# Delta rule inputs of a two-block model: two small sums computed with the data as moving columns in four column groups

## The chip, the cores and the metric

The kernel is one program on one core of a Trainium2 chip. The metric is the device time of one execution in microseconds (us); the median of several executions is what is compared. TensorE is called PE below, VectorE DVE, ScalarE ACT, GpSimd POOL, and the sync engine, which issues the weight loads, SP.

## The reference, cut to what matters

The reference is a block of two layers followed by a second block of two layers, on 256 tokens of width 1024. The part that matters here is the gated delta rule in the second layer of the first block:

```
proj = xn @ od_w_in[i]                       # 1024 -> 3080 columns
z, qkv, gate, b_raw, a_raw = jnp.split(proj, OD_SPLITS, axis=-1)   # b_raw, a_raw: 4 columns each
qkv = jax.nn.silu(causal_dwconv(qkv, conv_w))
q = l2norm(split_heads(q, DN_HEADS, DN_HEAD_DIM)) * DN_HEAD_DIM ** -0.5   # 4 heads of 128 channels
k = l2norm(split_heads(k, DN_HEADS, DN_HEAD_DIM))
beta = jax.nn.sigmoid(b_raw)
g = -jnp.exp(a_log) * jax.nn.softplus(a_raw + dt_bias)
o = chunked_gated_delta_rule(q, k, v, g, beta)
# l2norm(t) = t * rsqrt(sum(t * t, axis=-1) + 1e-6)
```

Two small results are at stake. The first is `xn @ od_w_in[:, 3072:3080]`, eight columns per token, the raw beta and decay inputs. The second is the sum of squares over the 128 channels of each head of q and of k, eight numbers per token.

## The kernel before

Activations lie channel-major: `xnT` is 8 tiles of 128 channels by 256 tokens, `d_cv` is 12 such tiles (4 of q, 4 of k, 4 of v). Tokens come in two tiles of 128 (`t` in `range(TT)`). Results that are needed per token as a scalar (beta, decay, norms) lie with the token on the partition, in the small table `small`.

Large products go through the weights in units of 4096 columns, loaded by SP into a ring of two places, and each unit in pieces of 512 columns. For each piece ACT writes a rounded copy (`w_hi`, `round_weights`), POOL writes the remainder (`w_lo`, `remainders`), and PE multiplies high by high, low by high, and, after the remainder is there, high by low. Four pieces are held at once (`HELD`), and ACT may round piece p only when PE has started piece p - 3 (`piece_started`). The units around the change are, in this order, `odq`, `odk`, `odv` (channel-major, the inputs of q, k and v), then `ozv`, `ozu`, `odg` (token-major). In the token-major routine `split_token_major` the argument `second_half` is work put in before piece 2, and `after` is work put in before piece 4.

Each engine's program is written out by hand in one order, and engines wait for each other by semaphores: `B.take` waits until a PSUM bank is emptied, `B.wait_full` until PE has filled it, and `DA`/`DV` name steps of ACT and DVE. Around the change the orders are:

- PE: `odk`, the 16 matmuls "ba" (8 moving columns each, L1198, into bank 4), 4 transposes of the spatial gating weights (L1203, bank 5), `odv`, `ozv` pieces 0 to 3, `square_sums` (16 matmuls of one moving column, L1162, bank 4, and 4 of eight, "gc", L1167, bank 5), `ozv` pieces 4 to 7, `ozu` pieces 0 and 1, `rows_a` (L1175, waits for DVE's step "diag_a"), and on.
- ACT: `odv` pieces 0 to 2, silu of q (`silu(0)`, L1922), `last_tap(1)` (the convolution's last tap of k, read from PSUM through L1670), the sigmoid of beta (L1936), `odv` pieces 3 to 7, `silu(1)`, `ozv` 0 and 1, the pieces of the softplus (L1942 to L1948) with `ozv` 2 and 3 between, `last_tap(2)`, `ozv` 4 to 6, the copies of "gc" (L1954), the logarithm of the sums of squares (L1956, step "rates"), `ozv` 7, `ozu` 0, the exponential of the factors (L1962, which waits for DVE's step "logs"), `ozu` 1 and on.
- DVE: `convolution(1)` (L2514 scales the banks, L2521 adds three taps, 12 instructions), the shift of the decay input, the masked spatial weights, the squares of q and k (L2544, step "squares"), the decay g, `convolution(2)`, then the sums of squares plus epsilon (L2552), and a chain of small operations to the step "logs" (L2567).

In both small sums the data is the stationary operand: a 128x128 tile of `xnT` or of `d_sq` is loaded into PE, and the 8 weight columns or one column of ones move through it. So each result lands with tokens on partitions. All these are full float32 matmuls, and the profile keeps two records for each.

## Time and profile before

| what | us |
|---|---|
| three executions | 2037.42, 2040.48, 2041.2 |
| their median | 2040.48 |
| the profiled execution | 2043.08 |
| its span in the trace | 2041.3 |
| PE busy in it | 2003.6 |
| POOL busy in it | 1621.6 |
| ACT busy in it | 1088.5 |
| DVE busy in it | 862.6 |
| "ba" matmuls (L1198), busy | 4.7 |
| squares matmuls (L1162), busy | 3.6 |

The trace spans 2041.3 us of the 2043.08 us that this execution took, so 1.8 us lie around it. A PE row's length is from issue to the modelled end, so rows that follow each other overlap; the distance between the starts of two rows is what a row costs when PE never waits. The granted clock of PE is 1.00 where it runs at 2.4 GHz and 0.50 at 1.2 GHz; over the span it is 0.992.

### The profile page before, as it was taken

The numbers are of one execution on the slowest core, as the hardware profiler recorded it, in microseconds if no ns is written. First come the engines' busy times: TensorE is split into PE (matmuls) and PEld (weight loads), VectorE is DVE, ScalarE is ACT, GpSimd is POOL, SyncE is SP. The second block draws the span as 40 slices with busy tenths as digits, with TensorE's granted clock in tenths as the row PEclk, the third lists the DMA queues.
The fourth block names the chain that finished last, engine by engine and source line by source line (L and its number), as shares of the span: only waits on it lengthen the run. The fifth ranks groups of instructions, "written<-read, shape, count | busy, mean of one in ns | idle before, by whom it ended". The sixth has DMA issues, their size and how long they took to land.

```text
span 2041.3 us, 32301 instructions
## 1 busy us (share of the span) xinstructions
PE 2003.6 (98%) x12383; PEld 1752.5 (86%) x12383; DVE 862.6 (42%) x2024; ACT 1088.5 (53%) x2124; POOL 1621.6 (79%) x1272
## 2 busy tenths in 40 slices
PE   9999999999999999999999989999999999999998
PEld 8798999898888999898788858888997788678886
DVE  4412565056522466082413273553432412644541
ACT  4454666456354566444554585544444544865443
POOL 6685898977395898999889518999997896268997
PEclk9999999999999999999999999999999999999999
DMA  9753555553053676565456604655554557135553
GB/s 308 149 181 123 186 186 176 184 172 104 21 186 124 198 234 199 181 191 186 145 183 192 209 2 165 204 188 186 183 189 145 165 188 231 63 125 175 190 200 107
DMA packets 244271, 343.14 MB, mean 168 GB/s; under 512 B 8819, under 2 KB 172755, under 8 KB 243989
## 3 DMA queue, kind: packets, MB, share of 16 engines
q1 hardware_dynamic: 231832, 330.83, 49.2%
q10 hardware_dynamic: 12285, 10.24, 2.5%
q8 instruction: 99, 1.62, 0.3%
q14 instruction: 55, 0.45, 0.1%
HBM read 336.85 MB, written 4.19 MB: 167 GB/s over the span
## 4 chain that ended last, share of the span: by engine, by line
PE 90%; DVE 3%; ACT 3%; POOL 1%; issue 1%; DMA 1%; DVEq 0%; POOLq 0%; SPq 0%; ACTq 0%
PE bank L774 9%; PE bank L781 9%; PE bank L777 9%; PE bank L824 8%; PE bank L830 8%; PE bank L827 8%; PE bank L796 7%; PE bank L854 5%; PE bank L857 5%; PE bank L861 5%; PE bank L801 4%; DVE E L2305 1%; POOL w_lo L1572 1%; PE bank L1367 1%; DVE E L2291 1%
## 5 line engine op out<-in xcount | busy, mean ns | idle before, releaser
L1572 POOL TENSOR_TENSOR w_lo<-ring,w_hi 128x512 fp32r<-128x512 f32 (+1 forms) x1216 | 1575.1, 1314 | 368.0 <-ACT w_hi L1670 330.4
L1670 ACT ACTIVATE w_hi<-ring 128x512 fp32r<-128x512 f32 (+1 forms) x1216 | 757.8, 630 | 786.2 <-PE bank L824 261.5
L774 PE MATMUL bank<-x_pair,w_hi 128*128 128x256 f32 x1504 | 380.7, 285 | 2.3 <-DVE x_pair L2191 1.5
L777 PE MATMUL bank<-x_pair,w_hi 128*128 128x256 f32 x1504 | 378.0, 283 | 0.0
L824 PE MATMUL bank<-w_hi,x_pair 128*128 128x512 f32 (+1 forms) x752 | 299.4, 398 | 2.9 <-issue 1.9
L827 PE MATMUL bank<-w_hi,x_pair 128*128 128x512 f32 (+1 forms) x752 | 293.8, 391 | 0.0
L774 PEld LDWEIGHTS bank<-x_pair,w_hi 128*128 128x128 f32 x1504 | 289.4, 192 | 5.0 <-issue 1.5
L777 PEld LDWEIGHTS bank<-x_pair,w_hi 128*128 128x128 f32 x1504 | 289.4, 192 | 0.4
L781 PE MATMUL bank<-x_pair,w_lo 128*128 128x256 f32 x1504 | 242.1, 283 | 0.0
L830 PE MATMUL bank<-w_lo,x_pair 128*128 128x512 f32 (+1 forms) x752 | 232.7, 391 | 1.4 <-POOL w_lo L1572 1.3
L781 PEld LDWEIGHTS bank<-x_pair,w_lo 128*128 128x128 f32 x1504 | 207.9, 192 | 0.0
L854 PE MATMUL bank<-w_hi,hidden 128*128 128x512 f32 x480 | 187.2, 390 | 0.0
L857 PE MATMUL bank<-w_hi,hidden 128*128 128x512 f32 x480 | 186.8, 389 | 0.0
L796 PE MATMUL bank<-x_pair,w_hi 128*128 128x512 f32 x640 | 174.7, 394 | 0.0
L824 PEld LDWEIGHTS bank<-w_hi,x_pair 128*128 128x128 f32 x752 | 144.2, 192 | 32.9 <-issue 5.4
L830 PEld LDWEIGHTS bank<-w_lo,x_pair 128*128 128x128 f32 x752 | 142.6, 192 | 33.0 <-POOL w_lo L1572 4.3
L827 PEld LDWEIGHTS bank<-w_hi,x_pair 128*128 128x128 f32 x752 | 144.2, 192 | 27.8 <-issue 0.7
L861 PE MATMUL bank<-w_lo,hidden 128*128 128x512 f32 x480 | 147.8, 389 | 0.0
L796 PEld LDWEIGHTS bank<-x_pair,w_hi 128*128 128x128 f32 x640 | 109.4, 189 | 14.7
L2183 DVE TENSOR_TENSOR h<-bank,h 128x512 f32<-128x512 f32 x36 | 23.1, 685 | 209.4 <-PE bank L861 153.6
L801 PEld LDWEIGHTS bank<-x_pair,w_lo 128*128 128x128 f32 x640 | 98.2, 189 | 13.6
L854 PEld LDWEIGHTS bank<-w_hi,hidden 128*128 128x128 f32 x480 | 90.1, 188 | 18.8 <-issue 0.4
(333 smaller groups left out, 2422.0 us busy)
## 6 DMA issues: line engine op xcount, KB each, us to landing
ring<-in_w_in SPq DMA_DIRECT2D x74, 1024.0 KB, 5.0
ring<-in_ffn_w_up SPq DMA_DIRECT2D x44, 1024.0 KB, 5.1
ring<-in_w_ffn_in SPq DMA_DIRECT2D x44, 1024.0 KB, 5.1
ring<-in_ffn_w_down SPq DMA_DIRECT2D x20, 1024.0 KB, 4.9
ring<-in_w_ffn_out SPq DMA_DIRECT2D x20, 1024.0 KB, 5.0
ring<-in_xattn_wkv SPq DMA_DIRECT2D x16, 1024.0 KB, 5.3
ring<-in_w_o_ret SPq DMA_DIRECT2D x16, 1024.0 KB, 5.0
ring<-in_od_w_in SPq DMA_DIRECT2D x12, 1024.0 KB, 5.2
```

The costliest lines, as they stand in the source:

```text
L774: m = mm(out_, view(w_hi)[:, k, :], x_hi[:, 4 * kh + k, :], start=start, stop=False)
L777: mm(out_, view(w_hi)[:, k, :], x_lo[:, 4 * kh + k, :], start=False, stop=False)
L781: m = mm(out_, view(w_lo)[:, k, :], x_hi[:, 4 * kh + k, :], start=False, stop=stop)
L796: m = mm(bank[b][:, :], view(w_hi)[:, k, :], x_pair[:, 4 * kh + k, :, :].rearrange("p a n -> p (a n)"), start=kh == 0 and k == 0, stop=False)
L824: m = mm(acc, hi, view(w_hi), start=k == 0, stop=False)
L827: mm(acc, lo, view(w_hi), start=False, stop=False)
L830: m = mm(bank[b0 + t][:, 0:n], x_hi[:, k, t * P:(t + 1) * P], view(w_lo), start=False, stop=k == KT - 1)
L854: m = mm(bank[b][:, :], hi, view(w_hi), start=kt == 0, stop=False)
L857: mm(bank[b][:, :], lo, view(w_hi), start=False, stop=False)
L861: m = mm(bank[b][:, :], x_hi[:, kt, t * P:(t + 1) * P], view(w_lo), start=False, stop=kt == tiles - 1)
L1572: tt(view(w_lo), src, view(w_hi), ALU.subtract).then_inc(w_lo_ready, 1)
L1670: return A(o, i_, ACT.Copy, **kw)
```

## The change

Both sums are turned round: the data moves, the small operand is stationary. A stationary tile of 32 columns fills one of the four column groups of PE, so that its result lands on 32 partitions of the bank (partitions 32c to 32c+31 for group c), 256 tokens wide. Eight channel tiles go through in two rounds of four groups, and the second round adds to the first.

- "ba": 8 matmuls of 32 stationary by 256 moving columns ("baT", L1209 in the new numbering) leave four partial sums in bank 4. ACT copies the bank to `d_baT` (which lies in `d_kb`, unused at that point). After the 4 transposes of the spatial weights, 2 matmuls (L1219) take `d_baT` as stationary and a matrix `fold`, which has a one for every partition with the same number modulo 32, as 8 moving columns: this adds the four groups and turns the result to tokens on partitions, in the layout of before.
- squares: 8 matmuls ("ssT", L1164) with a 32-column window of `sel` that holds a single column of ones, so that group c gets the sums of head c of q on its first partition and of k on its second. They are issued before `ozv` piece 2 in place of piece 4. ACT copies the bank to `d_ssT` between `ozv` piece 3 and `last_tap(2)`. Before piece 4 PE transposes the two halves back (L1172), and "gc" follows as before. DVE then reads the eight columns with a stride, in two instructions for one (L2581).
- DVE fills `sel` and the spare columns of `wba` at the start and builds `fold` from the identity by three additions in the first layer. `wba` and `sel` take 96 more float32 columns of SBUF.

```diff
-        wba = sb("wba", [P, KT, 8])
+        wba = sb("wba", [P, KT * 8 + 32])
+        sel = sb("sel", [P, 64])
...
+        d_ssT, d_baT = (d_kb[:, 2 * j:2 * j + 2, :].rearrange("p a b -> p (a b)") for j in range(2))
+        fold = sel[:, 40:48]
...
             def square_sums():
                 pe.wait_ge(*DV.after("squares"))
+                B.take(pe, "ssT", 4)
+                for r in range(2):
+                    for c in range(4):
+                        m = mm(bank[4][32 * c:32 * c + 32, 0:SEQ], sel[:, 1 - r:33 - r], d_sq[:, 4 * r + c, :], start=r == 0, stop=r == 1)
+                m.then_inc(full[4], 1)
+            def turn_sums():
+                B.wait_emptied(pe, "ssT")
                 B.take(pe, "ss", 4)
-                for a in range(8):
-                    for t in range(TT):
-                        c = (a // 4) * 8 + t * 4 + a % 4
-                        m = mm(bank[4][:, c:c + 1], d_sq[:, a, t * P:(t + 1) * P], c_ones[:, 0:1], start=True, stop=True)
+                for t in range(TT):
+                    m = tr(bank[4][:, t * P:(t + 1) * P], d_ssT[:, t * P:(t + 1) * P], ident[:, :])
                 m.then_inc(full[4], 1)
...
-            B.take(pe, "ba", 4)
-            for t in range(TT):
-                for k in range(KT):
-                    m = mm(bank[4][:, t * 8:(t + 1) * 8], xnT[:, k, t * P:(t + 1) * P], wba[:, k, :], start=k == 0, stop=k == KT - 1)
+            B.take(pe, "baT", 4)
+            for r in range(2):
+                for c in range(4):
+                    k = 4 * r + c
+                    m = mm(bank[4][32 * c:32 * c + 32, 0:SEQ], wba[:, 8 * k:8 * k + 32], xnT[:, k, :], start=r == 0, stop=r == 1)
             m.then_inc(full[4], 1)
...
+            B.wait_emptied(pe, "baT")
+            B.take(pe, "ba", 4)
+            for t in range(TT):
+                m = mm(bank[4][:, t * 8:(t + 1) * 8], d_baT[:, t * P:(t + 1) * P], fold, start=True, stop=True)
+            m.then_inc(full[4], 1)
             channel_major("odv", x_parts)
-            token_major("ozv", x_parts, after=square_sums)
+            token_major("ozv", x_parts, second_half=square_sums, after=turn_sums)
...
             silu(0)
+            evacuate("baT", d_baT)
             last_tap(1)
...
             round_weights("ozv", HELD - 1, HELD)
+            evacuate("ssT", d_ssT)
             last_tap(2)
...
-            ts(small[:, 20:22, :].rearrange("p a b -> p (a b)"), bank[4][:, 0:16], EPS, None, ALU.add).then_inc(empty[4], 1)
+            sums_of = bank[4][:, 0:SEQ].rearrange("p (t a j) -> p t a j", t=2, a=4)
+            for r in range(2):
+                m = ts(small[:, 20 + r, :].rearrange("p (t a) -> p t a", t=2), sums_of[:, :, :, r], EPS, None, ALU.add)
+            m.then_inc(empty[4], 1)
```

In the order listings below, line numbers of the new kernel are 3 higher than before in the piece routines (L777 is the old L774, L784 the old L781, L827, L830 and L833 the old L824, L827 and L830); a row's name is the tile, and a count with x says how often it follows itself.

PE between `odk` and `odv`, before:

```order
L781 MATMUL bank<-x_pair,w_lo 128x256 x3
L1198 MATMUL bank<-wba,xnT 128x8 [waits bank_empty4,xn_ready]
L1198 MATMUL bank<-wba,xnT 128x8 x15
L1203 MATMUL bank<-ident,PT 128x128 [waits params_loaded,bank_empty5]
L1203 MATMUL bank<-ident,PT 128x128 x3
L774 MATMUL bank<-x_pair,w_hi 128x256 [waits w_hi_ready,bank_empty2]
```

PE at the same place, now:

```order
L784 MATMUL bank<-x_pair,w_lo 128x256 x3
L1209 MATMUL bank<-xnT,wba 32x256 [waits bank_empty4,xn_ready]
L1209 MATMUL bank<-xnT,wba 32x256 x7
L1214 MATMUL bank<-ident,PT 128x128 [waits params_loaded,bank_empty5]
L1214 MATMUL bank<-ident,PT 128x128 x3
L1219 MATMUL bank<-sel,region 128x8 [waits bank_empty4]
L1219 MATMUL bank<-sel,region 128x8
L777 MATMUL bank<-x_pair,w_hi 128x256 [waits w_hi_ready,bank_empty2]
```

Sixteen matmuls of 8 columns became eight of 256 in front of the transposes and two of 8 behind them, and those two wait for ACT's copy (`bank_empty4`).

PE between `ozv` piece 3 and piece 4, before:

```order
L830 MATMUL bank<-w_lo,x_pair 128x512 [waits w_lo_ready]
L830 MATMUL bank<-w_lo,x_pair 128x512
L1162 MATMUL bank<-region 128x1 [waits bank_empty4,dn_dve_steps]
L1162 MATMUL bank<-region 128x1 x15
L1167 MATMUL bank<-small,region 128x8 [waits bank_empty5,dn_dve_steps]
L1167 MATMUL bank<-small,region 128x8 x3
L824 MATMUL bank<-w_hi,x_pair 128x512 [waits w_hi_ready]
```

PE between `ozv` piece 1 and piece 2, now:

```order
L833 MATMUL bank<-w_lo,x_pair 128x512 [waits w_lo_ready]
L833 MATMUL bank<-w_lo,x_pair 128x512
L1164 MATMUL bank<-region,sel 32x256 [waits bank_empty4,dn_dve_steps]
L1164 MATMUL bank<-region,sel 32x256 x7
L827 MATMUL bank<-w_hi,x_pair 128x512 [waits w_hi_ready]
```

PE between `ozv` piece 3 and piece 4, now:

```order
L833 MATMUL bank<-w_lo,x_pair 128x512 [waits w_lo_ready]
L833 MATMUL bank<-w_lo,x_pair 128x512
L1172 MATMUL bank<-ident,region 128x128 [waits bank_empty4]
L1172 MATMUL bank<-ident,region 128x128
L1177 MATMUL bank<-small,region 128x8 [waits bank_empty5,dn_dve_steps]
L1177 MATMUL bank<-small,region 128x8 x3
L827 MATMUL bank<-w_hi,x_pair 128x512 [waits w_hi_ready]
```

The wait for the squares (`dn_dve_steps`) moved two pieces forward, and two transposes stand where sixteen one-column matmuls stood.

ACT from the silu of q to the sigmoid of beta, before:

```order
L1922 ACTIVATE region<-region 128x1024 [waits dn_dve_steps]
L1670 ACTIVATE region<-bank,vecs 128x256 [waits dn_dve_steps]
L1670 ACTIVATE region<-bank,vecs 128x256 x3
L1936 ACT_TABLE_LOAD
L1936 ACTIVATE small<-bank,rstd 128x4 [waits bank_full4]
```

ACT at the same place, now (L1938 is the old L1922, L1686 the old L1670, L1953 the old L1936):

```order
L1938 ACTIVATE region<-region 128x1024 [waits dn_dve_steps]
L1794 ACTIVATE region<-bank 128x256 [waits bank_full4]
L1686 ACTIVATE region<-bank,vecs 128x256 [waits dn_dve_steps]
L1686 ACTIVATE region<-bank,vecs 128x256 x3
L1953 ACT_TABLE_LOAD
L1953 ACTIVATE small<-bank,rstd 128x4 [waits bank_full4]
```

The copy of the new sums stands in front of the last tap of k.

## Rows read from the trace of the kernel before

**Rows 1.** The page's shares of the chain that ended last.

```profile
PE 90%; DVE 3%; ACT 3%; POOL 1%; issue 1%; DMA 1%; DVEq 0%; POOLq 0%; SPq 0%; ACTq 0%
```

**Rows 2.** PE's timeline, "ba" to `odv` piece 4: start, us, engine, line, operation, tiles, shape, count.

```profile
430.96 4.74 PE L1198 MATMUL bank<-wba,xnT 128*128 128x8 f32 x32
435.55 1.09 PE L1203 MATMUL bank<-ident,PT 128*128 128x128 f32 x4
436.30 0.56 PE L774 MATMUL bank<-x_pair,w_hi 128*128 128x256 f32 x1
...
443.80 0.28 PE L774 MATMUL bank<-x_pair,w_hi 128*128 128x256 f32 x1
```

**Rows 3.** Windows: stretch, us, busy of PE, PEld, DVE, ACT, POOL, clock, DMA, GB/s.

```profile
433.30:440.10 6.80, 6.80 (x34) 6.80 (x34) 6.20 (x17) 3.08 (x6) 1.28 (x1) 0.50 0.04 7
...
460.50:464.00 3.50, 3.50 (x10) 2.75 (x9) 2.73 (x13) 3.46 (x6) 1.37 (x2) 0.51 0.00 0
1112.00:1122.00 10.00, 9.71 (x98) 8.61 (x97) 1.34 (x2) 4.03 (x7) 7.66 (x7) 1.00 0.64 201
```

**Rows 4.** PE's timeline at a burst of 16 matmuls with 32 stationary columns (L1390).

```profile
1115.34 0.64 PE L781 MATMUL bank<-x_pair,w_lo 128*128 128x256 f32 x4
1115.91 1.93 PE L1390 MATMUL bank<-ring,E 128*32 128x256 f32 x32
1118.13 0.36 PE L774 MATMUL bank<-x_pair,w_hi 128*128 128x256 f32 x1 [0.29 <-issue]
```

**Rows 5.** ACT's timeline, last tap of k (in brackets the idle time before).

```profile
431.89 1.57 ACT L1670 ACTIVATE region<-bank,vecs 128x256 f32<-128x256 f32 x4 [0.48 <-DVE bank L2514]
```

**Rows 6.** PE's timeline from `ozv` piece 0 to `rows_a`, beginnings of pieces.

```profile
449.56 0.40 PE L824 MATMUL bank<-w_hi,x_pair 128*128 128x512 f32 x1
...
452.61 0.39 PE L824 MATMUL bank<-w_hi,x_pair 128*128 128x512 f32 x1
...
455.33 3.63 PE L1162 MATMUL bank<-region 128*128 128x1 f32 x32
458.82 1.04 PE L1167 MATMUL bank<-small,region 128*128 128x8 f32 x8
459.71 0.49 PE L824 MATMUL bank<-w_hi,x_pair 128*128 128x512 f32 x1
...
465.50 0.39 PE L824 MATMUL bank<-w_hi,x_pair 128*128 128x512 f32 x1
...
466.87 0.39 PE L824 MATMUL bank<-w_hi,x_pair 128*128 128x512 f32 x1
...
469.59 1.88 PE L1175 MATMUL bank<-region 128*128 128x512 f32 x4
```

**Rows 7.** DVE's timeline: taps of k, squares, taps of v.

```profile
433.50 5.10 DVE L2521 SCALAR_TENSOR_TENSOR region<-bank,vecs,region 128x255 f32<-128x255 f32 x12 [1.64 <-ACT region L1670]
...
447.16 2.29 DVE L2544 TENSOR_TENSOR region<-region 128x2048 f32<-128x2048 f32 x1 [7.13 <-ACT region L1922]
...
457.24 5.10 DVE L2521 SCALAR_TENSOR_TENSOR region<-bank,vecs,region 128x255 f32<-128x255 f32 x12 [1.64 <-ACT region L1670]
```

**Rows 8.** ACT's timeline: `ozv` pieces 4 to 6, piece 7 with `ozu` 0, `ozu` 1 and 2.

```profile
457.08 1.68 ACT L1670 ACTIVATE w_hi<-ring 128x512 fp32r<-128x512 f32 x3
...
463.00 1.13 ACT L1670 ACTIVATE w_hi<-ring 128x512 fp32r<-128x512 f32 x2
...
466.58 0.22 ACT L1962 ACTIVATE small<-small 128x24 f32<-128x24 f32 x1 [1.15 <-DVE small L2567]
466.71 1.14 ACT L1670 ACTIVATE w_hi<-ring 128x512 fp32r<-128x512 f32 x2
```

**Rows 9.** POOL's timeline, the remainders of the same pieces.

```profile
457.80 3.76 POOL L1572 TENSOR_TENSOR w_lo<-ring,w_hi 128x512 fp32r<-128x512 f32 x3 [3.43 <-ACT w_hi L1670]
463.69 2.54 POOL L1572 TENSOR_TENSOR w_lo<-ring,w_hi 128x512 fp32r<-128x512 f32 x2 [2.13 <-ACT w_hi L1670]
467.41 4.88 POOL L1572 TENSOR_TENSOR w_lo<-ring,w_hi 128x512 fp32r<-128x512 f32 x3 [1.18 <-ACT w_hi L1670]
```

More of the change, by code:

```diff
@@ L1515, in load_constants @@
                 sp.dma_start(e_poolw, I["pool_w"][0].rearrange("g c d -> c g d")).then_inc(const_loads, 16)
-                sp.dma_start(wba[:, :, :], I["od_w_in"][0][:, 3072:3080].rearrange("(k p) n -> p k n", p=P)).then_inc(const_loads, 16)
+                sp.dma_start(wba[:, 0:KT * 8].rearrange("p (k n) -> p k n", n=8), I["od_w_in"][0][:, 3072:3080].rearrange("(k p) n -> p k n", p=P)).then_inc(const_loads, 16)
                 sp.dma_start(dn_row[:, 0, :], I["dn_dt_bias"].broadcast_to([P, 4])).then_inc(const_loads, 16)
@@ L2340, in _ @@
             nc.vector.memset(nothing[:, :].bitcast(F32), 0.0).then_inc(nothing_ready, 1)
+            nc.vector.memset(wba[:, KT * 8:KT * 8 + 32], 0.0)
+            nc.vector.memset(sel[:, :], 0.0)
+            drain()
+            nc.vector.memset(sel[:, 1:2], 1.0)
             nc.vector.memset(cmpbias[:, 0, CMP_SEEN:N_CMP, :].rearrange("p b c -> p (b c)"), -FAR)
@@ L2371, in _ @@
             tt(g_both[:, :], vecs[:, r0:r0 + KT], vecs[:, r1:r1 + KT], ALU.mult)
+            tt(fold, ident[:, 0:8], ident[:, 32:40], ALU.add)
+            drain()
+            tt(fold, fold, ident[:, 64:72], ALU.add)
+            drain()
+            tt(fold, fold, ident[:, 96:104], ALU.add)
             for t in range(TT):
```

## The prediction

> **What bounds the kernel now.** I read the chain that ended last first: PE holds 90% of it [rows 1], so a microsecond that PE saves counts if nothing else steps in. Then I read PE's timeline around the two sums. The sum "ba" takes from 430.96 to 435.55, so 4.59 us, and the transposes 0.75 us more, until `odv` piece 0 at 436.30 [rows 2]. The sum of squares takes from 455.33 to 458.82, 3.49 us, and "gc" 0.89 us, until `ozv` piece 4 at 459.71 [rows 6]. Third, the windows of the granted clock: it is 0.50 (1.2 GHz) from 433.3 to 440.1 and 0.51 from 460.5 to 464.0 [rows 3]. So PE falls to its lower level 2.3 us after "ba" begins, and again right behind the squares and "gc": both times PE had done matmuls with 1 or 8 moving columns for more than 2 us, and it rose again only after dense work. What the falls cost: `odv` pieces 0 to 3 take from 436.30 to 443.80, 7.50 us [rows 2], where the next four take 5.76 us, from 443.80 to 449.56 [rows 2, 6], that is 1.44 each. So 1.74 us are lost. `ozv` pieces 4 to 6 take 5.79 us from 459.71 to 465.50, where a piece at full clock takes 1.37 (465.50 to 466.87) [rows 6]. So 1.68 us are lost.
>
> Fourth, I read who else is close behind. ACT and DVE go through a long chain for the delta rule in the same stretch: its steps are paced by each other and not by PE. That chain decides how much of PE's saving stays.
>
> **What a burst in four column groups costs.** The trace has the same form, 128 by 32 stationary and 256 moving columns in float32, at L1390: 16 matmuls, 32 records. The piece before it has its last four matmuls from 1115.34, at 0.12 us each (a piece of 1.44 us has twelve), so PE would have gone on at 1115.82; it goes on with the next piece at 1118.13 [rows 4]. The 16 cost 2.31 us, of which 1.93 us lie in the records, 0.06 us each, and some 0.4 us are the gaps ahead of and behind them. Eight matmuls with their 16 records cost 2.31 - 0.96, so 1.35 us. The Trainium skill (TensorEngine Tiling (Array Packing), Key Properties) says that a change of tiling mode drains TensorE; the trace agrees, with gaps of 0.09 and 0.29 us. The clock stays at 1.00 over the ten microseconds around this burst [rows 3], so I take the new bursts as no cause of a fall.
>
> **First place, "ba".** New times in before's own scale. PE starts baT at 430.96 and is free for the transposes at 432.3. These took 0.75 us at half clock [rows 2]; at full clock at least half of that, and I take 0.45, to 432.75. ACT is free at 431.41 (it idled 0.48 us before 431.89) [rows 5] and copies the bank when it is full, at about 432.4; 256 columns take it 0.39 us (1.57 for four) [rows 5], so until 432.8 to 432.9. There the fold starts: it has four records, and "gc" has eight in 0.89 us [rows 6], so 0.45 us. With 0.1 us for the hand-over PE starts `odv` at 433.45 in place of 436.30: 2.85 us earlier. The transposes hide all but 0.1 to 0.2 us of the round trip over ACT; without that cover it would cost 0.5 us more. With a clock that doesn't fall, `odv` piece 4 starts 5.76 us later, at 439.2 in place of 443.8. **The first place gives 2.85 + 1.74, so 4.6 us** at `odv` piece 4.
>
> The copy stands ahead of the last tap of k, which ends at 434.5 in place of 433.46, so the taps of k on DVE (5.1 us) [rows 7] end near 439.6, 1 us later. Who waits for that is the silu of k. ACT reaches it behind `odv` piece 7, which is tied to the start of `odv` piece 4 and so comes near 440.2. It is on time with 0.6 us to spare. The sigmoid of beta follows 1 us later, and ACT then rounds `odv` piece 3 until 436.7, where PE asks for it at 433.45 + 4.32, so 437.8. Both fit.
>
> **Second place, the squares.** From `odv` piece 4 on (call its start S, 443.80 before) ACT's and DVE's chain keeps its distances: `odv` piece 7, silu of k, `ozv` 0 and 1, softplus, decay, taps of v, logarithm. So I count from S. The squares are ready at S + 5.65 (447.16 + 2.29) [rows 7] and PE asks for them at `ozv` piece 2, S + 8.8 (452.61) [rows 6], with 3.2 us to spare. PE does the burst until S + 10.15, pieces 2 and 3 until S + 12.9, two transposes in 0.25 (about half of the four above), "gc" in 0.89, and starts piece 4 at S + 14.05, where it was S + 15.9; its high part is there at 457.08 + 0.56, S + 13.84 [rows 8], and for its remainder (457.80 + 1.25, S + 15.25) [rows 9] PE waits 0.3 us. ACT's copy of ssT falls in a wait of ACT for the scaled bank of v, and costs nothing. PE asks for piece 7 at S + 18.45 (three pieces of 1.37 on, and the 0.3). But ACT rounds piece 7 behind the logarithm, which needs the sums plus epsilon, which DVE does behind the taps of v (457.24 to 462.3) [rows 7]: the high part is there at 463.00 + 0.56, S + 19.76 [rows 8], and the remainder at 463.69 + 1.27, S + 21.16 [rows 9]. None of that comes sooner by the change; the earlier "gc" and the second DVE instruction (under 0.2 us) about cancel. PE waits 1.3 us for the high part and, after its four high matmuls of 0.91 us, 0.5 us for the remainder. It starts `ozu` at S + 21.65, where it was S + 23.07 [rows 6]: 1.4 us earlier. `ozu` piece 0 ends at S + 23.0. Piece 1 is rounded behind the exponential that waits for DVE's "logs", at 466.71 + 0.57, S + 23.5 [rows 8], and its remainder comes at 467.41 + 1.3 to 1.6, S + 24.9 to 25.2 [rows 9]. PE waits 0.5 and then 0.5 to 0.8 us and reaches `rows_a` at S + 25.35 to 25.7, where it was S + 25.79 (469.59) [rows 6]. **So the second place gives 0.1 to 0.44, I take 0.35 us.** Of its 1.85 us of direct saving and 1.68 us of clock nearly all becomes waiting.
>
> **The rest.** The fills of `sel` and `fold` lie where DVE waits for PE in the first layer, and cost nothing there. Behind `rows_a` DVE's, ACT's and PE's work have all moved by 4.6 to 5, so nothing new waits. **Sum: 4.6 + 0.35, so 5.0 us.** The profiled execution (2043.08, of which 2041.3 is the span) would become 2038.1. The three executions have a median 2.6 us below it, and I make the sum against that median too: 2040.48 - 5.0, so 2035.5 us. A spread of 3.8 us between them says that the time at the lower clock isn't the same in each; where the fall was shorter, less can be won.
>
> **Rivals.**
>
> *PE is the bound all through.* If ACT's and DVE's chain comes sooner than I count (its order leaves some starts to PE), the second place gives 3.49 - 1.35 - 0.25 = 1.89 us and 1.68 us of clock. Together 4.6 + 3.6 = 8.2 us, 2032.3 us. For it speaks that PE hardly idles in the stretch; against it, the time of rounding of piece 7, 1.9 us ahead of its use before (463.56 against 465.50) [rows 6, 8], less than what is saved. 15%.
>
> *The clock falls at the first place all the same.* PE goes 2.5 us without a dense piece, and the fall before came 2.3 us after "ba" began. Then `odv` starts at 433.7 and runs at half speed for half to all of the 6.4 us up to 440.1, which loses 1.6 to 3.2 us. At S 2.6 + 1.74 - 1.6 to 3.2, so 1.1 to 2.7 us are left, with the second place 1.5 to 3.1: 2037.4 to 2039.0 us, I take 2038.4. Against it stands the burst at L1390, 2.3 us long and with the clock at 1.00 [rows 3, 4]. The Trainium skill (TensorE: Matmul & The Clock Gate, Part 4: PE-mode transpose) says that a transpose doesn't count as busy for the clock; that would speak for this rival, since four of them stand between the burst and the fold. By that rule the time is this rival's, by the rows of L1390 the forecast's. 17%.
>
> *Slower, from the moved tiles.* `wba` and `sel` push all that is allocated behind them (the region with the attention's and the delta rule's tiles, `hidden`) by 96 float32. If ACT and DVE work on moved tiles became slower, it would show in the 6% of the chain that are theirs [rows 1], 122 us: 4% of it cancels the gain, and 8% costs 9.8 us, so 4.8 us net, 2045.3 us. The ring, `w_hi` and `w_lo`, on which the pieces rest, are allocated ahead of `wba` and don't move, and 384 bytes keep every alignment up to 128. 4%.
>
> **How the numbers follow.** The forecast has 64%. Differences under 0.2%, 4.1 us, can't be told from no change here. The forecast is 5.0 us, close to that line, with 1 us of doubt in its terms and the spread of the executions on top: 46 of its 64 I count as faster, 18 as the same. The first rival is faster (15), the second the same but for 2 (15 and 2), the third slower (4). So faster 0.63, same 0.33, slower 0.04. The range runs from under the first rival (2031.5) to above the upper end of the second (2039.4).
>
> **What would show it.** Right: the two bursts of 16 records last 1 us each and `odv` piece 0 starts 2.9 us sooner with the clock at 1.00 up to the end of `ozv`; PE rows of `ozv` piece 7 and `ozu` piece 1 name ACT or POOL as what ended 0.5 to 1.4 us of idle time; `rows_a` comes some 5 us sooner and everything after it by as much. Wrong: a clock of 0.5 anywhere from 430 to 470; no idle time in front of `ozv` piece 7 (the first rival); PE waiting in front of the fold, or for the squares at `ozv` piece 2; attention's DVE and ACT rows of the second block longer than before.

## The result

| | median us | lowest to highest | executions |
|---|---|---|---|
| kernel before | 2040.48 | 2035.28 to 2043.26 | 11 |
| changed kernel | 2044.73 | 2042.27 to 2046.59 | 11 |

The ratio is 1.0027, with a 95% interval of 1.0017 to 1.0037: the change makes the kernel slower by 3.5 to 7.5 us. The forecast was 2035.5 us in a range of 2031.5 to 2039.4, so the sign is wrong. What makes this case worth reading is that nearly every row which the prediction told the reader to look at came out as forecast. The loss is in other places.

**The two places of the change.** This is PE's timeline of the changed kernel around "ba", the rows that answer to [rows 2] (start, us, engine, line, operation, tiles, shape, count, idle time before and what ended it):

```profile
430.99 1.07 PE L1209 MATMUL bank<-xnT,wba 128*32 128x256 f32 x16
431.99 0.66 PE L1214 MATMUL bank<-ident,PT 128*128 128x128 f32 x4
432.65 0.58 PE L1219 MATMUL bank<-sel,region 128*128 128x8 f32 x4
433.09 0.36 PE L777 MATMUL bank<-x_pair,w_hi 128*128 128x256 f32 x1
...
444.68 0.40 PE L827 MATMUL bank<-w_hi,x_pair 128*128 128x512 f32 x1
```

The burst takes 1.0 us (430.99 to 431.99), the transposes 0.66, the fold 0.44, one right behind the other, and `odv` begins 2.10 us after the burst's start, where it took 5.34. The first piece of `ozv` starts at 444.68 in place of 449.56, 4.9 us sooner. And further on, what answers to [rows 6]:

```profile
448.02 1.07 PE L1164 MATMUL bank<-region,sel 128*32 128x256 f32 x16
449.02 0.50 PE L827 MATMUL bank<-w_hi,x_pair 128*128 128x512 f32 x1
...
451.88 0.38 PE L1172 MATMUL bank<-ident,region 128*128 128x128 f32 x2
452.09 0.96 PE L1177 MATMUL bank<-small,region 128*128 128x8 f32 x8
453.04 0.50 PE L827 MATMUL bank<-w_hi,x_pair 128*128 128x512 f32 x1
...
454.41 0.74 PE L833 MATMUL bank<-w_lo,x_pair 128*128 128x512 f32 x2 [0.18 <-POOL w_lo L1588]
...
458.81 0.50 PE L827 MATMUL bank<-w_hi,x_pair 128*128 128x512 f32 x1 [0.89 <-ACT w_hi L1686]
...
460.17 0.73 PE L833 MATMUL bank<-w_lo,x_pair 128*128 128x512 f32 x2 [0.16 <-POOL w_lo L1588]
...
462.52 0.50 PE L827 MATMUL bank<-w_hi,x_pair 128*128 128x512 f32 x1 [0.25 <-ACT w_hi L1686]
...
464.02 0.73 PE L833 MATMUL bank<-w_lo,x_pair 128*128 128x512 f32 x2 [0.31 <-POOL w_lo L1588]
464.59 1.88 PE L1185 MATMUL bank<-region 128*128 128x512 f32 x4
```

The waits in front of `ozv` piece 7 (ACT, then POOL) and of `ozu` piece 1 (ACT, then POOL) are the ones that the prediction names, and `rows_a` comes at 464.59 in place of 469.59: 5.0 us sooner, as summed. On ACT's timeline, what answers to [rows 8]: `ozv` piece 7 with `ozu` 0, and `ozu` 1 and 2, are rounded 4.86 us sooner than before each:

```profile
458.14 1.14 ACT L1686 ACTIVATE w_hi<-ring 128x512 fp32r<-128x512 f32 x2
...
461.85 1.14 ACT L1686 ACTIVATE w_hi<-ring 128x512 fp32r<-128x512 f32 x2
```

The windows of the clock, which answer to [rows 3] (stretch, us, busy of PE, PEld, DVE, ACT, POOL, clock, DMA, GB/s), hold no fall:

```profile
430.00:445.00 15.00, 14.99 (x131) 14.03 (x131) 9.37 (x19) 12.75 (x23) 11.02 (x9) 1.00 0.49 158
445.00:470.00 25.00, 23.04 (x111) 15.89 (x110) 19.26 (x39) 19.78 (x33) 16.79 (x13) 1.00 0.38 129
```

**Where the time went.** 5.0 us sooner at 464.59, and yet a span of 2042.6 us against 2041.3. So something of 6.3 us or more lies elsewhere. To find it I paired the two traces: ACT writes 1216 rounded pieces in both kernels, in the same order, and the start of the same piece (from the span's start) can be compared all through. A difference that stays level means that nothing differs in between. This table is worked out from those starts, in us. Its last two columns, e1 and e2, are the first two experiments below: the changed kernel with `hidden` at its old address, and the kernel before with `hidden` moved.

```
time in before   changed - before   e1 - before   e2 - before
141 us                -1.91            -2.34         -0.52
330                   -1.47            -2.33         -0.12
396                   -0.22            -2.33          1.12
576                   -5.06            -7.26         -0.37
803                   -4.54            -7.28          0.15
905                   -3.13            -7.28          1.55
1019                  -3.11            -7.31          1.56
1130                  -1.51            -7.49          3.19
1390                  -2.13            -8.63          1.97
1492                  -0.79            -8.57          3.52
1609                  -0.77            -8.57          3.54
1715                   0.41            -8.57          4.64
1873                  -0.57           -10.31          3.16
end of span            1.3            -10.0           4.5
```

The changed kernel loses 0.4 to 1.6 us at a time, in eight steps (in front of 330, 330 to 396, 576 to 803, 803 to 905, 1019 to 1130, 1390 to 1492, 1609 to 1715, and behind 1873). What it gains away from the two places is time at the lower clock: the granted clock was 0.50 for 3.4 us near 51 us and near 1730 us in this execution, where the kernel before's trace has 6.8 us at both. The steps lie where PE multiplies with a stationary tile out of `hidden`: the down projections, and the products that keep their left operand in parts of `hidden`. Those are eight stretches of 96, 192 or 264 such matmuls, and a stretch of 264 costs 1.3 to 1.5 us. The change doesn't touch the code of any of these. The view of one line shows what is different. First the kernel before, then the changed kernel, the low-by-high matmuls of the down projections (count, duration in ns as minimum/median/maximum, first and last start in us):

```profile
L857 PE MATMUL bank<-w_hi,hidden x480: 389/389/398, 345.8 to 2031.9; 128*128 128x512 f32 x160
```

```profile
L860 PE MATMUL bank<-w_hi,hidden x480: 387/395/405, 344.4 to 2032.9; 128*128 128x512 f32 x160
```

The same 480 matmuls take 395 ns in place of 389 in the median. From the page of the profile, the high-by-low ones, with the mean (busy us, mean ns, idle time before), before and changed:

```profile
L861 PE MATMUL bank<-w_lo,hidden 128*128 128x512 f32 x480 | 147.8, 389 | 0.0
```

```profile
L864 PE MATMUL bank<-w_lo,hidden 128*128 128x512 f32 x480 | 150.5, 395 | 0.0
```

Idle time is 0.0 in both, so this isn't a wait: each matmul is longer. Since these run back to back, I took the distance from one start to the next over the 1624 of them that the trace has (three lines of 480 and three of 64, less a few records): 226.9 ns on average before, 232.5 ns in the changed kernel. The difference of 5.6 ns times 1624 is **9.1 us**. With the operand out of `x_pair` the distance is the same in both (228.1 and 228.0). So -5.0 at the two places and +9.1 here give +4.1, and the measured medians differ by 4.25. For the two traces there is a third term: outside the two places the clock was low for 6.6 us less in the changed kernel's, which at half speed is 3.3 us, and 4.1 - 3.3 is 0.8 where the spans differ by 1.3.

The chain that ended last, by the page of the profile, answers to [rows 1]. It has the three `hidden` lines with 5% each, as before, and the shares hardly show the loss: 9.1 us are 0.4% of the span.

```profile
PE 89%; DVE 4%; ACT 3%; POOL 1%; issue 1%; DMA 1%; DVEq 0%; POOLq 0%; SPq 0%; ACTq 0%
```

What the change does to `hidden` is one thing: `wba` grows by 32 float32 and `sel` adds 64, so `hidden` and `region`, allocated behind them, lie 96 float32 (384 bytes) further on, while `w_hi`, `w_lo` and `x_pair` stay. In the built program of the kernel before, `hidden` begins 87040 bytes behind `w_hi` in each partition, which is 340 times 256; `w_lo` lies 8192 bytes behind `w_hi`, and `x_pair` 16384 bytes ahead of it, multiples of 256 too. The unused tile `line_rest` (8 columns), which the kernel before has in front of `region`, completes that multiple. In the changed kernel the 87040 are 87424, 341.5 times 256.

### The profile page after: what moved, and what is told of

It reads as the page before. It is cut to its first block, busy times and chain, and to the rows that moved or that the text cites. A ratio compares the mean times of both kernels' runs of the same rounds, so it can differ in the third digit from the quotient of the medians.

```text
span 2042.6 us, 32263 instructions
## 1 busy us (share of the span) xinstructions
PE 2003.6 (98%) x12357; PEld 1740.8 (85%) x12357; DVE 865.1 (42%) x2031; ACT 1088.3 (53%) x2126; POOL 1620.8 (79%) x1272
## 4 chain that ended last, share of the span: by engine, by line
PE 89%; DVE 4%; ACT 3%; POOL 1%; issue 1%; DMA 1%; DVEq 0%; POOLq 0%; SPq 0%; ACTq 0%
PE bank L777 9%; PE bank L780 9%; PE bank L784 9%; PE bank L827 8%; PE bank L833 8%; PE bank L830 8%; PE bank L799 7%; PE bank L860 5%; PE bank L864 5%; PE bank L857 5%; PE bank L804 4%; DVE E L2323 1%; POOL w_lo L1588 1%; PE bank L1383 1%; DVE E L2309 1%
## 5 line engine op out<-in xcount | busy, mean ns | idle before, releaser
L1686 ACT ACTIVATE w_hi<-ring 128x512 fp32r<-128x512 f32 (+1 forms) x1216 | 757.9, 630 | 787.6 <-PE bank L827 259.5
L777 PE MATMUL bank<-x_pair,w_hi 128*128 128x256 f32 x1504 | 379.5, 285 | 1.3 <-DVE x_pair L2209 0.6
L827 PE MATMUL bank<-w_hi,x_pair 128*128 128x512 f32 (+1 forms) x752 | 298.6, 397 | 4.1 <-issue 1.9
L830 PE MATMUL bank<-w_hi,x_pair 128*128 128x512 f32 (+1 forms) x752 | 292.5, 389 | 0.0
L777 PEld LDWEIGHTS bank<-x_pair,w_hi 128*128 128x128 f32 x1504 | 288.4, 192 | 4.0 <-issue 2.0
L784 PE MATMUL bank<-x_pair,w_lo 128*128 128x256 f32 x1504 | 241.6, 283 | 0.0
L833 PE MATMUL bank<-w_lo,x_pair 128*128 128x512 f32 (+1 forms) x752 | 231.9, 390 | 2.4 <-POOL w_lo L1588 2.2
L784 PEld LDWEIGHTS bank<-x_pair,w_lo 128*128 128x128 f32 x1504 | 207.5, 192 | 0.0
L860 PE MATMUL bank<-w_hi,hidden 128*128 128x512 f32 x480 | 189.7, 395 | 0.0
L857 PE MATMUL bank<-w_hi,hidden 128*128 128x512 f32 x480 | 189.4, 395 | 0.0
L827 PEld LDWEIGHTS bank<-w_hi,x_pair 128*128 128x128 f32 x752 | 143.3, 191 | 35.2 <-issue 5.9
L833 PEld LDWEIGHTS bank<-w_lo,x_pair 128*128 128x128 f32 x752 | 140.9, 190 | 35.3 <-POOL w_lo L1588 7.2
L830 PEld LDWEIGHTS bank<-w_hi,x_pair 128*128 128x128 f32 x752 | 143.4, 191 | 27.6 <-issue 0.7
L864 PEld LDWEIGHTS bank<-w_lo,hidden 128*128 128x128 f32 x480 | 90.4, 188 | 21.2
```

Source lines behind the costliest of these rows:

```text
L777: m = mm(out_, view(w_hi)[:, k, :], x_hi[:, 4 * kh + k, :], start=start, stop=False)
L784: m = mm(out_, view(w_lo)[:, k, :], x_hi[:, 4 * kh + k, :], start=False, stop=stop)
L827: m = mm(acc, hi, view(w_hi), start=k == 0, stop=False)
L830: mm(acc, lo, view(w_hi), start=False, stop=False)
L833: m = mm(bank[b0 + t][:, 0:n], x_hi[:, k, t * P:(t + 1) * P], view(w_lo), start=False, stop=k == KT - 1)
L857: m = mm(bank[b][:, :], hi, view(w_hi), start=kt == 0, stop=False)
```

## The experiments

**Theory A**: the two sums give what was forecast, and the whole loss comes from the distance between `hidden` and the weight tiles. **Theory B**: the loss comes from the turned sums (their tiling mode, or later work that they disturb), and the longer matmuls only go along with it. **Theory C**: `hidden` is slower by its own new address, for example for want of some alignment, wherever the other operand is.

### The changed kernel with `hidden` at its old address

```diff
-        wba = sb("wba", [P, KT * 8 + 32])
-        sel = sb("sel", [P, 64])
+        sb("old_wba", [P, KT * 8])
 ...
         region = sb("region", [P, REGION])
+        wba = sb("wba", [P, KT * 8 + 32])
+        sel = sb("sel", [P, 48])
```

> The changed kernel with wba and sel allocated behind the region (sel cut to the 48 columns it uses) and a hole of 64 columns where wba was, so that dn_row, dn_g, hidden and the region stand where they stood before the change. Theory A (the move of hidden by 384 bytes costs all that was lost behind the delta rule: the matmuls with hidden as stationary operand start 227 ns apart before and 232 after): distance back to 227 ns in the down projections, 8.8 us less than the changed kernel, 2036 us, 0.2 to 0.3% faster than before. Theory B (the loss comes from the new instructions or their timing): as the changed kernel, 2044 to 2045 us, distance 232 ns.

Measured: 2034.25 us (2031.87 to 2036.46), a ratio of 0.9977 with an interval of 0.9965 to 0.9989 to the kernel before beside it (2038.37). The program of every engine is that of the changed kernel. The high-by-low row is back at its old value:

```profile
L865 PE MATMUL bank<-w_lo,hidden 128*128 128x512 f32 x480 | 147.8, 389 | 0.0
```

In the table above (column e1) its difference to before is level in all eight stretches in which the changed kernel loses. It falls at 396 to 576 (the two places, -4.9) and otherwise only where the granted clock was low for a shorter time in this execution (about 51, 1150 and 1730 us). The changed kernel's ratio divided by this one, 1.0027 / 0.9977, is 1.0050, so 10.2 us for 384 bytes, next to the 9.1 that the matmuls add up to. B falls.

### The kernel before, `hidden` moved by the same 384 bytes

```diff
         wba = sb("wba", [P, KT, 8])
+        sb("pad", [P, 96])
```

> The kernel before with nothing changed but 96 unused float32 columns allocated in front of dn_row, so that dn_row, dn_g, hidden and the region move by 384 bytes as in the changed kernel. Theory A: the distance between matmuls with hidden stationary becomes 231 to 240 ns, each down projection loses 1.4 us, in all 8 to 9 us, 2049 us. Theory B: no change, 2040 us, 227 ns.

Measured: 2048.5 us (2045.89 to 2053.35), ratio 1.0048 (1.0033 to 1.0063), so 6.7 to 12.8 us lost with nothing of the change in it. The same row:

```profile
L862 PE MATMUL bank<-w_lo,hidden 128*128 128x512 f32 x480 | 150.5, 395 | 0.0
```

The distance of starts is 232.5 ns, and its column in the table (e2) rises by the same steps as the changed kernel's (+1.24 from 330 to 396, +1.40 from 803 to 905, +1.63 from 1019 to 1130), and falls in between where its clock was low for a shorter time. The two effects multiply to what was measured: 0.9977 x 1.0048 = 1.0025, against 1.0027.

### Other distances

```diff
         sel = sb("sel", [P, 64])
+        sb("pad", [P, 32])
```

> The changed kernel with 32 more unused columns, so that hidden stands 512 bytes behind its old place in place of 384. Theory A in the form that only the place modulo 512 bytes counts: 227 ns and about 2036 us. If any move hurts: 232 ns and 2045 us. Theory B: 232 ns.

This is the changed kernel with `hidden` 512 bytes from its old place. One execution took 2035.8 us (before beside it: 2038.37 in the median), the distance of starts 226.9 ns. Then the kernel before with `sb("pad", [P, 64])`, `[P, 32]` and `[P, 16]` behind `wba`, so 256, 128 and 64 bytes:

> The kernel before with 64 unused columns in front of dn_row: hidden moves by 256 bytes. 384 bytes gave a distance of 232.6 ns and 512 bytes 226.9. If only a multiple of 512 bytes is right: 230 ns or more and up to 9 us slower. If a multiple of 256 is enough: 227 ns.

> The kernel before with 32 unused columns in front of dn_row: hidden moves by 128 bytes. If only a multiple of 256 bytes is free of cost, as 256 and 512 with 226.9 ns and 384 with 232.5 say: 232.5 ns and 9 us slower. If 384 bytes was a special case: 227 ns.

> The kernel before with 16 unused columns in front of dn_row: hidden moves by 64 bytes. If any distance that is no multiple of 256 bytes costs the same: 232.5 ns. If the cost grows with the misfit: less than at 128 bytes.

One execution of each took 2041.24, 2046.49 and 2052.0 us, beside 2040.59 for before with the first and 2040.63 with the others. The rows of the low-by-high line, in that order of kernels (256, 128, 64 bytes):

```profile
L858 PE MATMUL bank<-w_hi,hidden 128*128 128x512 f32 x480 | 186.8, 389 | 0.0
```

```profile
L858 PE MATMUL bank<-w_hi,hidden 128*128 128x512 f32 x480 | 189.6, 395 | 0.0
```

```profile
L858 PE MATMUL bank<-w_hi,hidden 128*128 128x512 f32 x480 | 190.4, 397 | 0.0
```

The distances of starts are 226.9, 232.5 and 233.3 ns. So shifts of 0, 256 and 512 bytes cost nothing, and 64, 128 and 384 bytes cost 5.6 to 6.4 ns for each matmul. With 64 bytes that explains 6.4 x 1624, so 10.4 us of the 11.4 measured. The traces of 64 and 128 bytes differ by 5.5 us in their spans: 1.3 are 0.8 ns for each of the 1624, and the clock was low for 32.5 us in all in the one and 24.7 in the other, which at half speed is 3.9 us. These are single executions, and a time of one can lie 5 us off by the clock alone; the distances of starts, each a mean over 1624 matmuls, are what carries this comparison.

### Which address counts

First everything moved together, `ring`, `x_pair`, the weight tiles and `hidden`; then only what lies from `w_hi` on, so that `x_pair` alone stays:

```diff
+        sb("pad", [P, 96])
         ring = sb("ring", [P, RING, UNIT])
```

> The kernel before with 96 unused columns in front of everything, so that the stationary tiles (x_pair, hidden) and the moving ones (w_hi, w_lo) all move by 384 bytes and keep their distance from each other. If what counts is the place of the stationary tile relative to the moving one: 227 ns everywhere and 2040 us. If the place of the stationary tile by itself counts: 232 ns for hidden and for x_pair too, some 30 us or more lost over all pieces. Theory B: 2040 us.

```diff
         x_hi, x_lo = x_pair[:, :, 0, :], x_pair[:, :, 1, :]
+        sb("pad", [P, 96])
         w_hi = sb("w_hi", [P, HELD, PIECE], F32R)
```

> The kernel before with 96 unused columns in front of w_hi: w_hi, w_lo and all behind them, hidden too, move by 384 bytes; ring, h, xnT and x_pair stay. If what counts is the place of the stationary tile relative to the moving w_hi and w_lo: hidden as stationary stays at 227 ns, and x_pair as stationary in the token-major products goes from 228 to about 232.5 ns, 2100 records, 9 to 10 us slower. If what counts is hidden's place by itself or relative to the ring: hidden goes to 232.5 ns and x_pair stays at 228.

All moved: one execution of 2042.4 us, in the spread of before's beside it (2034.45 to 2044.85). The distance is 226.9 ns with `hidden` and the same as in before with `x_pair`, and from 141 to 1873 us its difference to before's trace stays between -0.5 and -0.8 us, with none of the steps. That takes away theory C: `hidden` lies 384 bytes from its old address here too, and is as fast as ever. Weights moved: 2046.11 us against 2040.63. Here `hidden` moves together with `w_hi`, and it is the matmuls with `x_pair` that changed. Rows of the token-major lines by shape, in the kernel before:

```profile
L824 PE MATMUL bank<-w_hi,x_pair 128*128 128x512 f32 x720 | 287.5, 399 | 2.9 <-issue 1.9 <-DVE x_pair L2639 0.7 <-ACT w_hi L1670 0.3
L827 PE MATMUL bank<-w_hi,x_pair 128*128 128x512 f32 x720 | 282.3, 392 | 0.0
L777 PE MATMUL bank<-x_pair,w_hi 128*128 128x256 f32 x1504 | 378.0, 283 | 0.0
```

and with the weights moved:

```profile
L825 PE MATMUL bank<-w_hi,x_pair 128*128 128x512 f32 x720 | 291.6, 405 | 2.9 <-issue 1.9 <-DVE x_pair L2640 0.7 <-ACT w_hi L1671 0.3
L828 PE MATMUL bank<-w_hi,x_pair 128*128 128x512 f32 x720 | 285.4, 396 | 0.0
L862 PE MATMUL bank<-w_lo,hidden 128*128 128x512 f32 x480 | 147.9, 389 | 0.0
L778 PE MATMUL bank<-x_pair,w_hi 128*128 128x256 f32 x1504 | 375.0, 282 | 0.0
```

With `x_pair` stationary and the weights moving they cost more (228.1 to 232.8 ns from start to start); `hidden` keeps its 389. With the weights stationary and `x_pair` moving they cost a little less (119.8 to 118.8 ns over 5102 of them with 256 columns, 232.3 to 230.2 ns over 640 with 512). The sum is 2114 x 4.8 - 5102 x 1.0 - 640 x 2.1, so 3.7 us. The two traces differ by 3.0 us, of which the clock, low for 1.6 us less with the weights moved, explains 0.8. What decides is where the stationary and the moving tile lie to each other: 0 modulo 256 bytes in the kernel before, for `hidden` and for `x_pair`, and every layout that keeps it so has the short distance with 512 moving weight columns. PEld is busy for 86% of the span beside PE's 98%, so weights are loaded while the matmul before streams its columns; that the two reads meet in some part of SBUF is my reading of it, and no run shows where.

### One place at a time

Both with `hidden` at its old address; the edits are shown in part. In the first only "ba" is turned (the squares stand as in the kernel before, `sel` unused by them), in the second only the squares:

```diff
-            token_major("ozv", x_parts, second_half=square_sums, after=turn_sums)
+            token_major("ozv", x_parts, after=square_sums)
```

> As e1_same_place (everything behind wba at its old address), but only the sum ba is turned round; the squares are summed as before the change. By the steps of the prediction: 4.6 us at odv piece 4, so that this alone gives 4.2 to 4.6 us of the gain, 2034 to 2036 us against 2038 to 2040 before, and the clock still falls once behind the squares. If the first place gave only its direct part and the clock's share came back later: 2.9 us.

```diff
-            B.take(pe, "baT", 4)
+            B.take(pe, "ba", 4)
 ...
-            evacuate("baT", d_baT)
```

> As e1_same_place, but only the squares are turned round; ba stays as before the change. By the prediction ACT's and DVE's chain (taps of v, logarithm, rounding of ozv piece 7 and ozu piece 1) takes nearly all of it back: 0.1 to 0.44 us, no difference that can be measured, with idle time in front of ozv piece 7 that names ACT. If PE is the bound all through: 3.6 us less than before.

"ba" alone: 2038.0 us (2036.08 to 2040.0), ratio 0.9992 (0.9982 to 1.0003) to 2040.59 beside it. So it is 1.6 us faster by the ratio, at most 3.7, and the 4.2 to 4.6 us that I expected did not come. In its trace the rounding of the pieces is 4.7 us earlier than before's up to the squares. Then the 32 records of the one-column matmuls and "gc" follow, and the clock falls for longer than it did there before. PE's timeline, and the windows around:

```profile
451.27 3.63 PE L1166 MATMUL bank<-region 128*128 128x1 f32 x32
454.76 1.45 PE L1171 MATMUL bank<-small,region 128*128 128x8 f32 x8
```

```profile
451.20:455.20 4.00, 4.00 (x38) 3.96 (x37) 2.29 (x6) 3.12 (x7) 1.47 (x2) 1.00 0.80 266
455.20:462.00 6.80, 6.80 (x20) 5.54 (x20) 5.60 (x18) 5.47 (x8) 4.22 (x4) 0.50 0.00 0
```

So 6.8 us at 1.2 GHz, where before had 3.5 in [rows 3], and 3.1 of the 4.7 us are left. Squares alone: 2038.42 us (2035.41 to 2041.06), ratio 0.9990 (0.998 to 1.0). In its trace, PE's timeline and the windows around "ba" and beyond:

```profile
428.65 3.64 PE L1209 MATMUL bank<-wba,xnT 128*128 128x8 f32 x32
...
432.15 0.64 PE L1214 MATMUL bank<-ident,PT 128*128 128x128 f32 x4
```

```profile
428.60:432.20 3.60, 3.60 (x35) 3.60 (x35) 1.71 (x4) 3.10 (x6) 1.73 (x2) 1.00 0.71 270
432.20:440.00 7.80, 7.80 (x67) 7.80 (x67) 5.19 (x15) 4.49 (x9) 5.79 (x5) 1.00 0.42 134
```

Here the old "ba" ran its 32 narrow records and the clock didn't fall at all; it gains 3.1 us on before's trace at that point by this alone, and the turned squares add 0.0 to 0.3 us (0.95 us of idle time in front of `ozv` piece 7, 0.24 in front of `ozu` piece 1). So in this trace the squares are worth what was forecast, or less.

This trace also splits the first place. With the clock at 1.00 the old "ba" and the transposes take 3.9 us (428.65 to 432.54, where `odv` begins), the turned ones 2.1. So of the 4.9 us that the changed kernel gains there, 3.1 are clock and 1.8 are PE's shorter work.

How much of the medians is clock, one trace can't tell, but every execution has its mean granted clock on record. The kernel before has 0.9931 (mean of the 27 executions beside these two), "ba" alone 0.9935 (12), squares alone 0.9947 (11). The first experiment, with both sums turned, has 0.9962 (12) beside 0.9935 of before (21). If PE's time at 0.50 counts half, the differences are worth an estimated 0.8, 3.3 and 5.5 us, each give or take about 1. So "ba" alone on average hands back behind the squares what the clock gave it, as its trace shows. For the squares alone the estimate is above what the ratio gives (2.0 us), and for both together it is above the 4.7 us by which they are faster: part of what the clock gives becomes waiting too, as at the squares. So on this estimate the clock is worth as much as the whole gain. The traces fit this: with both sums old the clock fell at both places in seven traces of seven, with both turned at neither in four of four. The trace of the squares alone, in which the old "ba" drew no fall, is the exception that shows it to be a matter of the single execution.

### Rounding earlier on ACT

The turned sums leave PE waiting for rounded pieces. This is the first experiment's kernel with three pieces rounded ahead of the waits that ACT stands in:

```diff
+            round_weights("ozv", HELD + 3)
             B.wait_emptied(act, "ss")
 ...
-            round_weights("ozv", HELD + 3)
-            round_weights("ozu", 0, 1)
+            round_weights("ozu", 0, 3)
             act.wait_ge(*DV.after("logs"))
 ...
-            round_weights("ozu", 1, HELD - 1)
             silu(2)
```

> e1_same_place with ACT's order changed: ozv piece 7 is rounded before the logarithm of the squares and ozu pieces 1 and 2 before the exponential that waits for DVE. If the idle time of PE in the second place comes from that order, the wait in front of ozv piece 7 (0.9 us) and of ozu piece 1 (0.25 us) goes, rows_a comes up to 1.7 us sooner until it waits for DVE's diag_a, and the whole is 1 to 1.7 us under e1_same_place. If something else holds it: no difference.

Measured: 2034.38 us (2032.02 to 2036.07), ratio 0.9968 (0.9958 to 0.9979). It is the lowest of all ratios, but the first experiment's interval overlaps it and its median is 2034.25, so the 1 to 1.7 us that I expected aren't shown by the times. The waits for the high part in front of `ozv` piece 7 and `ozu` piece 1 are gone, and one larger has come in front of `rows_a`:

```profile
461.79 0.40 PE L828 MATMUL bank<-w_hi,x_pair 128*128 128x512 f32 x1
...
462.72 0.63 PE L834 MATMUL bank<-w_lo,x_pair 128*128 128x512 f32 x2
464.79 1.98 PE L1186 MATMUL bank<-region 128*128 128x512 f32 x4 [1.45 <-DVE region L2601]
```

The trace has 5.7 us against before's where the first experiment has 4.9, so 0.8 us is won. The rest of the idle time has moved: PE now waits for DVE in front of `rows_a`. That is what "nearly all becomes waiting" comes down to. DVE's chain sets when this stretch ends, and ACT's order only decides at which row PE waits for it.

## Why the prediction was wrong

**What bounds the kernel now** held: PE's own matmuls, down to 5.6 ns in one. With `hidden` at its old address the sum holds as well: 4.7 us by the ratio (2.2 to 7.1), where 5.0 were forecast.

**First place.** Forecast 2.85 us directly and 1.74 by the clock. The burst took 1.0 us where I took 1.35 from L1390, the rest 1.10 where I took 1.15, and `odv` started 3.2 us sooner. At `ozv` piece 0 it is 4.9 us, where 4.6 were forecast. The clock stayed at 1.00, with four transposes between burst and fold. The Trainium skill (TensorE: Matmul & The Clock Gate, Part 4: PE-mode transpose) says that a transpose doesn't count as PE-busy in the same way; the rival that I weighed for that reason didn't come, in five traces of five. What the prediction had mis-sized is the split: its "directly" holds "ba" and transposes that ran at half clock in part. The squares alone show 1.8 us direct and 3.1 by the clock, and "ba" alone shows that the clock's part stays only if the clock doesn't fall for longer at the squares.

**Second place.** Forecast 0.35, with 1.3 and 0.5 us of idle time at `ozv` piece 7 and 0.5 and 0.5 to 0.8 at `ozu` piece 1. The changed kernel's rows have 0.89 and 0.16, 0.25 and 0.31, with the same releasers. From `ozv` piece 0 to `rows_a` it took 19.91 us against 20.03: the place gave 0.1 us. That PE's saving becomes waiting was the right mechanism; the first wait is shorter than forecast because PE came to piece 7 at 457.9, where S + 18.45 is 457.4 in this trace (S is 438.92): pieces at 1.37 to 1.40 us and restarts after a wait added up to 0.5.

**The rest** is the step that failed. It puts everything outside the two places at nothing, for the reason that "The fills of `sel` and `fold` [...] cost nothing there" and "nothing new waits". No row speaks against either, but they asked the wrong question: no one waits, PE is slower at work that the diff doesn't touch. The third rival had the right trigger, the tiles that `wba` and `sel` push along, and drew two conclusions that fell. It looked for the price on ACT and DVE, in 6% of the chain, and not on PE, in 90%, although the page of the profile says that 3 x 480 matmuls with 512 columns read `hidden`. And it closed with "The ring, `w_hi` and `w_lo`, [...] don't move, and 384 bytes keep every alignment up to 128". That they don't move is what does the harm (all moved together: no cost; weights without `x_pair`: cost at `x_pair`), and an alignment to 128 bytes doesn't protect, since 128 bytes themselves cost 5.6 ns. The price that it missed is 1624 x 5.6 ns, 9.1 us, nearly twice the gain.

**The rivals.** PE as the bound all through is refuted by the idle time in front of `ozv` piece 7. The fall at the first place didn't come in any of the five traces with "ba" turned. Slower by moved tiles had 4% at 2045.3 us; the median is 2044.73, but by another mechanism at about the same price, which is luck. The numbers around the measured one fit: with the old distance the ratio is 0.9977, which by 2040.48 is 2035.8 us, and the forecast was 2035.5.

## What to carry to other kernels

A change that adds or grows a tile moves every tile allocated behind it. Where PE is the bound, list the pairs of stationary and moving tiles that straddle the new one, and either put new tiles behind all of them or keep their distances multiples of 256 bytes. Here the distances were such multiples before, shifts of 256 and 512 bytes cost nothing, and the multiple hung on a filler of 8 columns (`line_rest`) that looks like nothing in the source. The addresses in the built program show such a distance before anything is run. When every local row is as forecast and the total isn't, pair the starts of the same instruction in both traces: the steps in the difference name the code that lost, and the duration row of a line nobody touched gives the price.

## What the runs showed of the hardware

- The cost of a 128x512 matmul with a 128x128 stationary tile depends on where the two tiles lie to each other: 226.9 ns from start to start at shifts of 0, 256 and 512 bytes from before's layout, in which the distance is a multiple of 256 bytes, 232.5 at 128 and 384, 233.3 at 64. Moving both tiles by 384 bytes left it at 226.9. With `x_pair` moving and the weights stationary, a shift by 384 bytes made it cheaper instead, by 1.0 ns with 256 moving columns and 2.1 with 512.
- Sixteen records of 128 by 32 stationary and 256 moving columns in four column groups took 1.0 us twice, and the clock stayed at 1.00 behind them. The Trainium skill (TensorEngine Tiling (Array Packing), Key Properties) says that a change of mode drains TensorE; the traces show short gaps around each burst. By the starts of the records, four of them start 6 to 7 ns apart, and the next four 0.22 us behind them. The burst at 430.99 begins 0.09 us later than the piece before it leads one to expect, and what follows begins 0.11 us later; at the one at 448.02 it is 0.10 and 0.11. No run tells a change of mode from a change of shape here.
- A stretch of matmuls with 1 to 8 moving columns doesn't fetch the lower clock each time, nor for the same time. The same 32 records of "ba", 3.6 to 4.7 us long, came with 6.8 us at 0.50 in before's trace and with none in that of the squares alone; at the squares it was 3.5 us in before's and 6.8 with "ba" alone. Executions of the kernel before have mean clocks from 0.990 to 0.996 and times from 2034.45 to 2044.85 us, so an effect of a few us has to be read from the steps between two traces, or from many executions with their clocks.
